# The start of a merging phase reordered: context scans moved into the phase before, one operation folded away, a first product in two halves

## The reference

```python
def step(S, inp):                         # GLA state over chunks, one scan per direction
    a_n, dS_n = inp
    return a_n[..., None] * S + dS_n, S
...
inter = jnp.einsum('bhnid,bhnde->bhnie', q * jnp.exp(b), S_prev)
return (intra + inter).reshape(B, H, T, DV), S_fin
...
oc_gla, oc_gdn, ctx_states = run_mixers(p_c, None)        # context first
ox_gla, ox_gdn, _ = run_mixers(p_x, ctx_states)           # latents start from its final states
...
ya = rmsnorm(o_gla, gla_norm_g)... * jax.nn.silu(p['gla_g'])
yb = rmsnorm(o_gdn, gdn_norm_g)... * jax.nn.silu(p['gdn_g'])
x = x + gt1x * (jnp.concatenate([ya, yb], axis=-1) @ w_out)
```

## Time and profile before

| | |
|---|---|
| median of 3 runs | 1781.2 us (1779.32 to 1784.86) |
| the profiled execution's own time | 1786.23 us |
| its span, first to last instruction | 1784.4 us |
| TensorE busy | 1579.5 us, 89% of the span |
| VectorE, ScalarE, POOL busy | 57%, 36%, 24% |
| mean granted TensorE clock | 0.95 of full |
| merging | about 967 to 1102 us of the span |

### The profile page before, as it was taken

How to read it: one execution, slowest core, us unless ns; L and a number is a source line. 1 busy time by engine, 2 the same in 40 slices (tenths; PEclk the granted TensorE clock), 3 DMA queues, 4 the chain that set the end, 5 groups by cost and what they waited for, 6 DMA issues and landing times. The chain is left out here.

```text
span 1784.4 us, 35206 instructions
## 1 busy us (share of the span) xinstructions
PE 1579.5 (89%) x15022; PEld 1331.5 (75%) x15022; DVE 1015.5 (57%) x1542; ACT 640.9 (36%) x976; POOL 420.3 (24%) x369
## 2 busy tenths in 40 slices
PE   4599999999987878888876798799999989899997
PEld 1366887899987777777775687578888867787886
DVE  2534553101105777767676655845545588887975
ACT  3367436212112232222222323445545543233333
POOL 1301111111103555545544220422222200000000
PEclk7699999999998999989899899999999999999998
DMA  7213324336545433333322232044444487163422
GB/s 309 76 47 104 108 91 124 102 114 185 169 127 136 133 109 108 109 109 109 108 62 84 93 115 95 24 130 141 163 151 144 161 314 253 54 235 115 168 83 95
DMA packets 170269, 229.94 MB, mean 129 GB/s; under 512 B 34205, under 2 KB 102049, under 8 KB 169090
## 3 DMA queue, kind: packets, MB, share of 16 engines
q1 hardware_dynamic: 163602, 206.85, 35.9%
q0 software_dynamic: 6512, 20.84, 3.7%
HBM read 165.91 MB, written 61.73 MB: 128 GB/s over the span
## 5 line engine op out<-in xcount | busy, mean ns | idle before, releaser
L87 PE MATMUL fps<-xh_m,w1r_hi 128*128 128x512 f32 x448 | 177.5, 396 | 19.2 <-ACT s L2373 5.4
L87 PE MATMUL fps<-bh,ah 128*128 128x512 f32 x448 | 176.5, 394 | 14.3 <-DVE acc L2688 9.8
L88 PE MATMUL fps<-xl_m,w1r_hi 128*128 128x512 f32 x448 | 176.7, 394 | 0.0
L89 PE MATMUL fps<-xh_m,w1r_lo 128*128 128x512 f32 x448 | 176.4, 394 | 0.0
L89 PE MATMUL fps<-bh,al 128*128 128x512 f32 x448 | 175.7, 392 | 0.0
L88 PE MATMUL fps<-bl,ah 128*128 128x512 f32 x448 | 175.7, 392 | 0.0
L80 PE MATMUL ps_main<-hhi,whi 128*128 128x512 f32 (+3 forms) x360 | 137.0, 381 | 15.6 <-DVE wlo L694 11.7
L81 PE MATMUL ps_main<-hlo,whi 128*128 128x512 f32 (+3 forms) x360 | 133.5, 371 | 0.0
L82 PE MATMUL ps_main<-hhi,wlo 128*128 128x512 f32 (+3 forms) x360 | 133.4, 371 | 0.0
L2335 ACT ACTIVATE ah<-araw 128x2048 fp32r<-128x2048 f32 x28 | 53.7, 1918 | 186.0 <-PE fps L89 120.0
L80 PE MATMUL ps_main<-whi,hhi 128*128 128x256 f32 x416 | 120.2, 289 | 0.0
(11 more groups left out here) (304 smaller groups left out, 3575.0 us busy)
## 6 DMA issues: line engine op xcount, KB each, us to landing
s_hid<-hb SPq DMA_DIRECT2D x112, 256.0 KB, 2.3
araw<-s_hid SPq DMA_DIRECT2D x28, 1024.0 KB, 6.6
w1raw<-in_w_ff SPq DMA_DIRECT2D x16, 1024.0 KB, 6.2
w2b<-in_w_ff SPq DMA_DIRECT2D x16, 1024.0 KB, 6.9
raw<-in_w_in SPq DMA_DIRECT2D x14, 1024.0 KB, 5.3
wa<-in_w_ada SPq DMA_DIRECT2D x8, 1024.0 KB, 10.5
z_sb<-in_w_ada SPq DMA_DIRECT2D x16, 512.0 KB, 4.3
n_sb<-in_w_ada SPq DMA_DIRECT2D x16, 512.0 KB, 4.3
```

Source lines behind the costliest of these rows:

```text
L87: pe.matmul(out, lhi, rhi, start=start, stop=False, skip_group_check=True)
L88: pe.matmul(out, lhi, rlo, start=False, stop=False, skip_group_check=True)
L89: return pe.matmul(out, llo, rhi, start=False, stop=stop, skip_group_check=True)
```

## The change

Context scans: the three backward pairs and the copy go from the head of merging to the ends of mixing's steps 2, 3, 4 (`context_back`) and 5 (`context_end`). Merging's own scan counts start from zero.

VectorE's scans for the first three tiles come first in merging. The `tensor_scalar` behind the sum of squares is gone; its 1/P and EPS are the scale and a 128x1 bias of the Ln, and POOL fills that bias with a memset. POOL's order is `gate(0)`, `low_w(1)`, `gate(1)`, `low_w(3)`; block 5 goes to VectorE. ScalarE's and VectorE's first instructions are reordered. TensorE runs `inter(2)` ahead of the first product, and makes that product by halves of W_out's blocks: 0 to 3 for both column halves, `turn(1)`, then 4 to 7 for both.

```diff
@@ mixing, VectorE
+            def context_back(i):
+                to = 2 * TC - 2 - i
+                if i:
+                    dve.wait_ge(scan_back, 2 * i)
+                for a in R2:
+                    dve.scalar_tensor_tensor(K.ga_st[:, to, 1, a], K.ga_st[:, to + 1, 1, a], K.ga_a[:, to, 1, a:a + 1],
+                                             K.ga_st[:, to, 1, a], ALU.mult, ALU.add).then_inc(scan_back, 1)
+
+            def context_end():
+                dve.wait_ge(scan_back, 2 * (2 * TC - 1))
+                dve.tensor_copy(K.ga_st[:, 2 * NT, 1], K.ga_st[:, 0, 1])
...
                     advance(p)
+                    if TC <= p < 3 * TC - 1:
+                        context_back(p - TC)
+                    if p == 3 * TC - 1:
+                        context_end()
@@ merging, POOL
-            low_w(1)
-            gate(0)
-            low_w(3)
-            low_w(5)
-            gate(1)
+            pool.memset(eps[:], EPS).then_inc(eps_done, 1)
+            gate(0)
+            low_w(1)
+            gate(1)
+            low_w(3)
@@ merging, ScalarE
-                act.wait_ge(var_done, t + 1)
-                act.activation(lnv[:], var[:], ACT.Ln).then_inc(ln_done, 1)
+                act.wait_ge(ss_done, t + 1)
+                if t == 0:
+                    act.wait_ge(eps_done, 1)
+                act.activation(lnv[:], ss[:], ACT.Ln, scale=1.0 / P, bias=eps[:]).then_inc(ln_done, 1)
...
             for k in range(3):
                 high_w(k)
+            square(0)
             for x in range(2):
                 act.wait_ge(rows_done, x + 1)
                 act.activation(K.gt2[:, x * 512:(x + 1) * 512], ps_p[:, x], ACT.Copy).then_inc(row_out, 1)
-            square(0)
+            rsqrt(0)
+            square(1)
             high_w(3)
-            rsqrt(0)
             high_w(4)
+            high(0)
+            rsqrt(1)
             high_w(5)
-            square(1)
             high_w(6)
             high_w(7)
-            rsqrt(1)
-            high(0)
@@ merging, VectorE
-            def variance(t):
+            def squares_sum(t):
                 dve.wait_ge(sq_done, t + 1)
+                if t:
+                    dve.wait_ge(ln_done, t)
                 dve.tensor_reduce(ss[:], sq[:].rearrange("p (h n) -> p h n", n=P), AX.X, ALU.add).then_inc(ss_done, 1)
-                dve.wait_ge(ss_done, t + 1)
-                dve.tensor_scalar(var[:], ss[:], 1.0 / P, EPS, ALU.mult, ALU.add).then_inc(var_done, 1)
...
-            for i in range(2 * TC - 1):
-                advance(2 * TC - 2 - i, 2 * i)
-            dve.wait_ge(scan, CTX_SCANS - 1)
-            dve.tensor_copy(K.ga_st[:, 2 * NT, 1], K.ga_st[:, 0, 1]).then_inc(scan, 1)
             states(0)
+            states(1)
+            states(2)
+            add_states(0)
             low_w(0)
-            add_states(0)
-            states(1)
-            low_w(2)
-            variance(0)
+            squares_sum(0)
             add_states(1)
             scale(0)
+            low_w(2)
+            squares_sum(1)
+            low(0)
             low_w(4)
-            variance(1)
+            scale(1)
+            low_w(5)
             low_w(6)
-            low(0)
             low_w(7)
-            states(2)
-            scale(1)
@@ merging, TensorE
             inter(0)
             inter(1)
             turn(0)
+            inter(2)
+
+            def product(t, i, ks):
+                cs = slice(i * 512, (i + 1) * 512)
+                for k in ks:
+                    if t == 0 and i == 0:
+                        if k in (1, 3):
+                            pe.wait_ge(wo_lo_pool, (k + 1) // 2)
+                        else:
+                            pe.wait_ge(wo_lo_dve, (0, 2, 4, 5, 6, 7).index(k) + 1)
+                    last = mm3x(pe, ps_p[:, i], yhi[:, t % 2, k], ylo[:, t % 2, k], whi[:, k, cs], wlo[:, k, cs],
+                                k == 0, k == KT - 1)
+                return last
+
             pe.wait_ge(row_out, 2)
-            for t in range(TL):
+            pe.wait_ge(lo_done, 2)
+            product(0, 0, range(4))
+            product(0, 1, range(4))
+            turn(1)
+            product(0, 0, range(4, KT)).then_inc(p_ready, 1)
+            product(0, 1, range(4, KT)).then_inc(p_ready, 1)
+            for t in range(1, TL):
```

More of the change, by code:

```diff
@@ L1001, in mix_phase @@
         kin_sub, kin_exp, kin_done = m.sem("kin_sub"), m.sem("kin_exp"), m.sem("kin_done")
-        kt_ready, kt_out = m.sem("kt_ready"), m.sem("kt_out")
+        kt_ready, kt_out, scan_back = m.sem("kt_ready"), m.sem("kt_out"), m.sem("scan_back")
         gs_ready, gs_out, scan = two("gs_ready"), two("gs_out"), m.sem("gla_scan")
@@ L1753, in merge_phase @@
         sq = m.sb("msq", [P, D])
-        ss, var, lnv, rs = (K.spare[:, 32 + 8 * i:40 + 8 * i] for i in range(4))
+        eps = m.sb("meps", [P, 1])
+        ss, lnv, rs = (K.spare[:, 32 + 8 * i:40 + 8 * i] for i in range(3))
         yhi, ylo = m.sb("yhi", [P, 2, KT, P], F32R), m.sb("ylo", [P, 2, KT, P], F32R)
@@ L1762, in merge_phase @@
         inter_ready, o_done, sq_done, ss_done = m.sem("inter_ready"), m.sem("mo_done"), m.sem("msq_done"), m.sem("mss_done")
-        var_done, ln_done, rs_done = m.sem("mvar_done"), m.sem("mln_done"), m.sem("mrs_done")
+        eps_done, ln_done, rs_done = m.sem("meps_done"), m.sem("mln_done"), m.sem("mrs_done")
         gated, y_done = m.sem("gated"), m.sem("my_done")
@@ L1768, in merge_phase @@
             m.sem("mxss_done"), m.sem("mxvar_done"), m.sem("mxln_done"), m.sem("mxrs_done"), m.sem("mxn_done"))
-        CTX_SCANS = 2 * (2 * TC - 1) + 1
         def tile(t):
@@ L1959, in states @@
                 for to in ((top, top - 1) if t else (top - 1,)):
-                    advance(to, CTX_SCANS + 2 * (2 * NT - 1 - to))
+                    advance(to, 2 * (2 * NT - 1 - to))
             def normalise():
@@ L1998, in _ @@
                 if t + 2 < TL:
-                    variance(t + 2)
+                    squares_sum(t + 2)
                 output(t, 0)
@@ L2010, in inter @@
             def inter(t):
-                pe.wait_ge(scan, CTX_SCANS + 2 * (2 * NT - 1 - 2 * (tile(t) + TC)))
+                pe.wait_ge(scan, 2 * (2 * NT - 1 - 2 * (tile(t) + TC)))
                 pe.wait_ge(ld_qs[t % 2], 16 * (t // 2 + 1))
@@ L2050, in _ @@
                 for i in range(2):
[L2051 to L2062, removed]
+                    pe.wait_ge(K.x1_done, 2 * (t - 1) + i + 1)
+                    product(t, i, range(KT)).then_inc(p_ready, 1)
                     if i == 0 and t + 1 < TL:
```

## The result

The changed kernel takes 1772.1 us, median of 5 runs (1770.67 to 1774.1), against 1781.2 us before, now also of 5 runs (1779.32 to 1784.86). The ratio of the changed kernel's time to that of the kernel before is 0.9945, with a 95% interval of 0.9928 to 0.9962: faster by 9.1 us, where 9.2 us were forecast. That the two numbers agree says little yet, as the profile shows. The ratios of the later measurements leave out two slow executions that stand far from the rest, one of the kernel before at 1795.1 us and one of e2 at 3359.4 us.

A forecast was written before the change was run, and what follows sets the result against it. TensorE bounds settled tiles, but VectorE, partly waiting on POOL, bounds the ramp, where the gain lies. Terms of 0 in mixing, -9.2 us in the ramp and 0 after take 1781.2 to 1772.0 us, range 1768 to 1777.5.

The forecast's parts named there:

- Mixing at no cost: Mixing: a context-scan pair of 0.65 us, or the 0.29 us copy, hides in VectorE's 0.94 us wait for TensorE; cost 0.
- R4: Rival, chance 0.03: mixing scans uncovered, each of seven instructions waits for POOL, 17 us in all; 7.8 us slower, 1789.
- The small terms: Start of merging: POOL's memset takes 0 to 2.35 us, done in time; the Ln's bias column costs near 0.
- The port: Ramp: scale(0) waits behind POOL's low_w(1), some 3.3 us long; low_w(2) against gate(1) shifts low(0) by 2.2 us.
- R2's first case: Ramp rival, R2 in all 0.12: VectorE's scale(0) takes the port before low_w(1); inter(2) comes 1.2 us later.
- The transfer that is late next: Ramp: the third tile's query states, issued about 979.05, land after 4.8 us at 983.8 and release inter(2).
- The ramp's 9.2 us: Ramp: inter(2) starts at 983.8 instead of 992.99, 9.2 us earlier, and the first product follows 2.9 us behind.
- R1: Ramp rival, chance 0.14: query states land after 2.7 us and the clock rises earlier; gain 11 to 13 us, 1769.
- 0 after the ramp: Later tiles and MLP: inter(3) doesn't wait, the settled period runs as before and the shift carries through; term 0.
- R3: Rival, chance 0.09: something behind the first tile waits and gives the lead back; at most 5 us remain, about 1778.
- The halves at nothing: First product split by halves of W_out's blocks: later blocks are ready in time, cost 0, and the halves bring little.
- The sum: Whole kernel: 0 in mixing, -9.2 us in the ramp, 0 after it; median 1781.2 to 1772.0 us, chance 0.62.

The follow-up runs named there:

- e2: Changed kernel with the 128x1 bias tile allocated behind yhi and ylo instead of ahead: ratio to before 0.9946, merging 124.6 us, period 13.59 us.
- e1: Changed kernel again, no edit, in a later session: ratio to before 0.9979, merging 126.6 us, period 13.83 us.
- e6: e2 without the halves, the first product in its old order (all eight blocks per column half): merging 124.6 us.
- e7: e2 with the third tile's query states ahead of load_x(1) in SP's order: merging 125.7 us, first product 19.95 us behind merging's start.
- e5: Kernel before with one unused 128x1 tile allocated ahead of yhi, no instruction added: merging 136.7 us, period 13.83 us.
- e4: Kernel before with only the context scans and copy moved into mixing: ratio to before 1.0005, merging 134.2 us.
- e10: e8 plus VectorE's low_w(0) before add_states(0), low_w(2) behind low(0), third query states before x loads, inter(2) before turn(0): 1766.0 us, ratio 0.9921.
- e8: e2 with POOL's low_w(1) ahead of gate(0): merging 121.8 us, first product 16.01 us behind merging's start.

## Why the prediction was right, point by point

**Mixing at no cost: right.** In the profile after, VectorE's scans in step 4 and what follows:

```profile
723.65 0.61 DVE L1462 SCALAR_TENSOR_TENSOR ga_st<-ga_st,ga_a 128x128 f32<-128x128 f32 x2
724.68 1.13 DVE L1388 SCALAR_TENSOR_TENSOR rr<-pr,gt,vtn 128x128 f32<-128x128 f32 x4 [0.42 <-PE pr L1590]
```

The wait of 0.94 in the earlier trace rows has become 0.42: the pair sits in it, and TensorE is as late as it was: `residual` starts 2.28 us behind the first of the step's scans in both kernels. R4 didn't happen.

**The small terms: right.** The memset takes 0.10 us and is done 0.06 us into merging. The Ln with the bias column takes 0.30 us, where it took 0.21 without it, so the term taken as near 0 is 0.09 us.

**The port: right.** `scale(0)` was to take some 3.3 us behind `low_w(1)` and took 3.36. Of the two orders that I left open, POOL's `gate(1)` went ahead of VectorE's `low_w(2)`. R2's first case, VectorE passing POOL there, was seen in none of the profiles that I read for it (after, e1, e6, e7).

**The transfer that is late next: half right.** The query states landed 3.9 us after their issue in e1, where I took 4.8, and `inter(2)` started at 15.46 behind merging's start, where my sum has 16.3. But I took the transfer for the only bound; e7 shows `low(0)` beside it: with the transfer early, the product came only 0.65 us sooner.

**The ramp's 9.2 us: right in kind.** It measures 10.0 us with a full clock at merging's start (e1), 7.75 without (after). My sum took that clock from the one profile that I had. The earlier rise of the clock, R1, didn't come: in e1 `inter(2)` takes 2.96 us, ends at 981.83, 0.65 us behind `low(0)`, and the product follows it.

**0 after the ramp: wrong.** The term is 0.24 us a tile, 1.9 us over eight. "From there the settled period runs as before" rested on unchanged instructions, and they were unchanged. R3, a wait behind the first tile, is not what happened: the window of the settled tile is busy throughout, and its matmuls themselves are further apart. I had read the new 128x1 tile only as a memset and an operand, and not as something that stands ahead of `yhi` in the allocation. The Trainium skill, page "SBUF — State Buffer", section "Operand start alignment", calls its rules legal limits and says that nothing was timed there; the price here is from e2 and e5.

**The halves at nothing: right** (e6). **The sum** came out at 9.2 for 9.1 us by luck: 0.8 us more in the ramp, 1.9 us given back after it, and a first measurement that lies below what merging alone explains. That is 8.1 us, or a ratio of 0.9955, with the full clock at merging's start; the three measurements of the changed kernel, 0.9945, 0.9979 and 0.9937, have the mean 0.9954. What was right is the mechanism in the ramp and the size of its term. The forecast's own span was also mis-added: landing at 981.8 to 984.1 gives gains of 11.2 to 8.9 us, so 1770.0 to 1772.3 and not 1770.5 to 1773.5.

What stays open: whether a gain too small for this spread hides outside merging. Merging starts at 967.5 and 968.8 in the two profiles with the context scans in merging, and between 958.1 and 972.1, 964.3 in the mean, in the twelve with the scans in mixing. With that spread two profiles say nothing, but the full-clock steps, e4's ratio and its mixing time show no gain. Open too are what sets the clock at merging's start, and what about the place of `yhi` and `ylo` costs 6 ns a matmul.

## What to carry to other kernels

When VectorE and POOL both work on SBUF tensors, put POOL's work where VectorE has none that reads two of them, and look at each release: an instruction of POOL's that needs no wait started here before the VectorE instruction that its predecessor released. When an early product is brought forward, check that all its operands come forward with it; e10 lost 1.2 us to one that didn't. A small tile allocated ahead of a matmul operand can change the matmuls, as it did here: allocate it behind them, and compare a settled period before and after any edit. Read a gain of half a per cent from the phase that was edited, because the clock in another phase can move the span by more (mixing took 395.0 to 402.8 us in one kernel).

## What the runs showed of the hardware that I had not expected

- Displacing `yhi` and `ylo`, or `ylo` alone, by a 128x1 tile lengthens the mean distance of the product's 128x512 matmuls at the full clock from 0.227 to 0.233 us; the period goes from 13.59 to 13.83 us, in six profiles against eight. With `ylo` alone displaced, the matmuls that load `yhi` are slowed as well.
- Merging begins at a granted clock of 1.00 in nine profiles and at 0.50 in five, of the same or nearly the same program. For the changed kernel the low one puts the first product at 20.60 for 18.35 us; for the kernel before it costs nothing (28.17 in e5 for 28.35).
- With a gap of TensorE filled by 32 small matmuls (e10) the clock stayed at 1.00 through a ramp in which every other profile has a stretch at 0.50, of over 3 us in e8 and 20 in the profile before. One profile shows this.
- A VectorE operation on two SBUF tensors and a POOL operation took turns in the profile after, the waiting one going first each time: `scale(0)` takes 3.36 us behind `low_w(1)`, and 1.23 in e8, where `low_w(1)` is over before it. In the profile before, at 987.2, VectorE went twice in a row.
